# Moving single steps in the engines' order at seven places of a two-block, fp32-split transformer kernel

## What is computed

```python
gate_a, gate_b = jnp.split(jax.nn.sigmoid(gates + b_gate[l]), 2, axis=-1)       # block 1
merged = gate_a * (o_a @ w_proj_a[l]) + gate_b * (o_b @ w_proj_b[l])
...
u = rms_norm_2(h, mix_norm[l])                                                  # block 2, per layer
(z_s, xbc, dt_s, qkv, z_d, b_d, a_d, gate_s, gate_d) = jnp.split(u @ w_in[l], split_points, axis=-1)
y_s = mamba2_branch(z_s, xbc, dt_s, ...)     # softplus of dt_s, convolution, scan, gated norm
y_d = deltanet_branch(qkv, z_d, b_d, a_d, ...)   # l2_norm of q and k, delta rule, gated norm
merged = (jax.nn.sigmoid(gate_s) * (y_s @ ssm_w_branch[l])
          + jax.nn.sigmoid(gate_d) * (y_d @ dn_w_branch[l]))
```

## Time and profile before

| | us |
|---|---|
| runs: median (lowest, highest) | 2187.85 (2183.99, 2188.01) |
| the profiled execution, device time | 2184.31 |
| its span, first to last instruction | 2182.5 |
| TensorE busy | 2113.6 (97%) |
| TensorE weight loads busy | 1851.0 (85%) |
| VectorE busy | 1333.4 (61%) |
| ScalarE busy | 1150.2 (53%) |
| GpSimd busy | 67.8 (3%) |

### The profile page before, as it was taken

The page is one execution under the profiler, slowest core; times in us unless marked ns, Lnnn a source line. Parts: engine busy times, 40 slices in busy tenths (PEclk is TensorE's granted clock), DMA queues, the critical chain, the costliest instruction groups (busy, mean ns, idle before and its releaser), DMA issues.

```text
span 2182.5 us, 39373 instructions
## 1 busy us (share of the span) xinstructions
PE 2113.6 (97%) x15558; PEld 1851.0 (85%) x15558; DVE 1333.4 (61%) x1846; ACT 1150.2 (53%) x1713; POOL 67.8 (3%) x88
## 2 busy tenths in 40 slices
PE   7999999999999999989999999999999998999998
PEld 5888778888888988889998888888998888998887
DVE  3447565565557976667555556555897575756555
ACT  3554754454445576645445445444557663535444
POOL 1000000000000010100000000000001010000000
PEclk9999999999999999999999999999999999999999
DMA  9763255545554545322445555554454430355553
GB/s 389 297 235 117 97 181 192 185 165 201 183 191 138 190 151 176 120 79 86 180 180 200 190 181 187 186 181 156 171 177 152 156 118 37 141 188 189 182 188 125
DMA packets 53458, 373.09 MB, mean 171 GB/s; under 512 B 6320, under 2 KB 6448, under 8 KB 9424
## 3 DMA queue, kind: packets, MB, share of 16 engines
q1 hardware_dynamic: 47808, 342.00, 43.4%
q0 software_dynamic: 5520, 29.23, 3.9%
HBM read 370.10 MB, written 1.11 MB: 170 GB/s over the span
## 4 chain that ended last, share of the span: by engine, by line
PE 85%; DVE 6%; ACT 4%; issue 2%; DMA 1%; POOL 1%; SPq 0%; DVEq 0%; ACTq 0%; POOLq 0%
PE banks L558 14%; PE banks L560 13%; PE banks L559 13%; PE banks L511 9%; PE banks L513 9%; PE banks L512 9%; PE banks L614 4%; DVE LO L2139 2%; ACT HI L1524 1%; PE banks L668 1%; DMA ring<-in_w_stream 1%; PE banks L643 1%; PE banks L644 1%; PE banks L648 1%; PE banks L1298 1%
## 5 line engine op out<-in xcount | busy, mean ns | idle before, releaser
L1524 ACT ACTIVATE HI<-ring 128x1024 fp32r<-128x1024 f32 x606 | 625.8, 1055 | 717.0 <-PE banks L560 394.8
L2133 DVE TENSOR_TENSOR LO<-ring,HI 128x1024 fp32r<-128x1024 f32 x334 | 409.0, 1227 | 368.8 <-ACT HI L1524 368.5
L2139 DVE TENSOR_TENSOR LO<-ring,HI 128x2048 fp32r<-128x2048 f32 x134 | 307.3, 2293 | 206.7 <-ACT HI L1524 206.3
L511 PE MATMUL banks<-UH,HI 128*128 128x256 f32 x1456 | 423.7, 291 | 5.0 <-DVE LO L2139 5.0
L512 PE MATMUL banks<-UL,HI 128*128 128x256 f32 x1456 | 411.7, 283 | 0.0
L513 PE MATMUL banks<-UH,LO 128*128 128x256 f32 x1456 | 411.5, 283 | 0.0
L558 PE MATMUL banks<-HI,UH 128*128 128x512 f32 x896 | 349.1, 390 | 0.9 <-DVE UL L2146 0.9
L560 PE MATMUL banks<-HI,UL 128*128 128x512 f32 x896 | 348.7, 389 | 0.0
L559 PE MATMUL banks<-LO,UH 128*128 128x512 f32 x896 | 348.6, 389 | 0.0
L511 PEld LDWEIGHTS banks<-UH,HI 128*128 128x128 f32 x1456 | 278.6, 191 | 21.5 <-issue 14.9
L512 PEld LDWEIGHTS banks<-UL,HI 128*128 128x128 f32 x1456 | 278.9, 192 | 1.9 <-issue 1.7
(11 more groups left out here) (354 smaller groups left out, 2992.9 us busy)
## 6 DMA issues: line engine op xcount, KB each, us to landing
ring<-in_w_stream SPq DMA_DIRECT2D x315, 1024.0 KB, 4.8
ARENA<-in_ada_stream POOLq DMA_DIRECT2D x16, 1024.0 KB, 7.8
ARENA<-in_ada_stream SPq DMA_DIRECT2D x8, 1024.0 KB, 13.7
GRMS<-cum_rows POOLq DMA_DIRECT2D x16, 256.0 KB, 3.5
ARENA<-in_na_bias POOLq DMA_DIRECT2D x2, 1024.0 KB, 12.9
RMS<-cum_rows POOLq DMA_DIRECT2D x8, 256.0 KB, 3.6
RSTD<-cum_rows POOLq DMA_DIRECT2D x8, 256.0 KB, 3.7
ARENA<-in_ropes POOLq DMA_DIRECT2D x1, 1088.0 KB, 10.1
```

What stands on the lines that cost most here:

```text
L511: nc.tensor.matmul(out, lh, rh, start=start, stop=False, **kw)
L1524: nc.scalar.activation(HI[:, q % PARTS, at], ring[:, q % RING, at], ACT.Copy).then_inc(hi_ready, 1)
L2133: nc.vector.tensor_tensor(LO[:, q % PARTS, at], ring[:, q % RING, at], HI[:, q % PARTS, at].bitcast(F32), ALU.subtract).then_inc(lo_ready, 1)
L2139: nc.vector.tensor_tensor(LO[:, q % PARTS, :], ring[:, q % RING, :], HI[:, q % PARTS, :].bitcast(F32), ALU.subtract).then_inc(lo_ready, 2)
```

## The change

Seven stretches of the order are changed. No instruction is added or taken away; some stand elsewhere on their engine. Both layers of block 2 run the same code, so five of the seven occur twice.

```diff
@@ TensorE, block 1 @@
+            b1_half(14, 1)
             ada_columns(1)
-            b1_half(14, 1)
@@ ScalarE, block 1 @@
                     if k == 9:
                         open_gates(0, 5)
-                    if k == 10:
+                    if k == 11:
                         open_gates(5, 3)
-                    if k == 11:
-                        open_gates(8, 3)
             gate_rows(0)
             heads_high(2)
+            open_gates(8, 8)
             gate_rows(1)
-            open_gates(11, 5)
@@ ScalarE, mixer start (VectorE alike, between the product r_*e and the wait for Ln) @@
                 nc.scalar.activation(SMX[:, 7, 0:SP_COLS], pk2("a_log", 0, SP_COLS), ACT.Exp).then_inc(small_scalar, 1)
+                ahead(LQ_WIDE)
                 act.wait_ge(small_vector, 3 * l + 3)
@@ VectorE, convolution loop @@
                     for i in range(ROUND):
-                        split(Q_LAYERS + LQ_WIDE + i + PARTS, rounds + r)
                         convolve(ROUND * r + i, i % 2)
+                        split(Q_LAYERS + LQ_WIDE + i + 1 + PARTS, rounds + r)
@@ ScalarE, z panels @@
-                    if j in (3, 5):
-                        qk_root((j - 3) // 2)
+                    if j in (2, 5):
+                        qk_root(j // 4)
@@ VectorE, z panels @@
-                    if j in (3, 5):
-                        qk_reciprocal((j - 3) // 2)
                     if j >= 4:
                         qk_norm(j - 4)
+                    if j in (2, 5):
+                        qk_reciprocal(j // 4)
@@ VectorE, last gate panels @@
                 for j in range(4):
-                    scan_low(j)
-                    if j == 1:
+                    if j == 0:
                         dve.wait_ge(orms_ready, l + 1)
                         nc.vector.reciprocal(OROOT, OROOT).then_inc(or_ready, 1)
+                    scan_low(j)
...
+                    if j == 2:
+                        late_low(L_ZD + L_GATES - END_GATES + 2)
                 for j in range(4):
                     at = slice(2 * j, 2 * j + 2)
                     branch_low(8 + j, YDL[:, at, :], YDH[:, at, :], QKV[:, at, :])
-                    if j % 2:
-                        late_low(L_ZD + L_GATES - END_GATES + 2 + j // 2)
+                    if j == 3:
+                        late_low(L_ZD + L_GATES - END_GATES + 3)
```

More of the change, by code:

```diff
@@ L1857, in _ @@
                 for j in range(j0):
-                    ahead(LQ_WIDE + j)
+                    if j:
+                        ahead(LQ_WIDE + j)
                     conv_in(j, j % 2)
@@ L2638, in _ @@
                     for i in range(ROUND):
-                        split(Q_LAYERS + LQ_WIDE + i + PARTS, rounds + r)
                         convolve(ROUND * r + i, i % 2)
+                        split(Q_LAYERS + LQ_WIDE + i + 1 + PARTS, rounds + r)
                 def conv_panel(j):
-                    ahead(LQ_WIDE + j)
+                    if j > L_CONV - SCAN_CONV - ROUND:
+                        ahead(LQ_WIDE + j)
                     convolve_tile(j, j % 2, 0)
```

## The result

| | before | after |
|---|---|---|
| first set of runs: median (lowest, highest), us | 2185.92 (2183.52, 2188.01) | 2167.48 (2166.05, 2169.37) |
| ratio after to before, 95% interval | | 0.9917 [0.9903, 0.9932] |
| profiled execution: device time, span | 2184.31, 2182.5 | 2166.82, 2165.0 |
| TensorE busy, and span less busy | 2113.6, 68.9 | 2110.9, 54.1 |

The change makes the kernel 0.83% faster. (The kernel before has a lower median here than ahead of the prediction, since a fourth execution has joined the three.) Of the span's 17.5 us, 68.9 - 54.1 = 14.8 are idle time of TensorE and 2.7 are busy time, although its work is the same.

A forecast was written before the change was run, and what follows sets the result against it. The prediction took TensorE, busy 97% of the span, and its gaps as the bound. Gains of 2.85 us once and 4.98 per layer sum to 12.8 us (0.59%), giving 2173.5 us, range 2168.5 to 2180.

The forecast's parts named there:

- term 1: Modulation columns: 24 products of a half panel cover VectorE's copy TensorE waited for; gain 1.1 us, once.
- term 4: First q/k root: table load, root and reciprocal placed earlier, ending TensorE's 2.1 us wait; gain 2.1 us per layer.
- term 7: LO part of gate panel E4 on VectorE placed earlier, so TensorE starts E4 sooner; gain 1.44 us per layer.
- Term 3: Softplus: Ln and Sigmoid with their table loads go behind HI of c2, which starts earlier; gain 1.24 us per layer.
- Term 2: Gates: sigmoids moved later, so copies for value products and broadcast, and UL, come earlier; gain 1.75 us, once.
- term 6: Reciprocal of OROOT comes earlier, its 0.7 us wait goes, but TensorE waits 0.5 at E2; gain 0.2 per layer.
- term 5: Second q/k root: VectorE's reciprocal and norm product swapped, but the broadcast needs both; the 1.2 us wait stays, gain 0.
- successor was late: Rival: ScalarE's drain at c2 and the LO of P0 each come 0.8 us later; 2176.8 us, 17%.
- The convolution stayed TensorE's: Rival: the reordered loop's branch makes VectorE set the convolution's pace, 17.3 us lost; 2192.3 us, 2%.
- The swap: Rival: swapping reciprocal and product at the second q/k root gains 1.2 us twice; 2171.1 us, 6%.
- Longer low stretches: Rival: the clock's low stretches come out longer in three places by 1.7 us; 2178.6 us, 10%.
- the table loads at double cost: Rival: moved ScalarE table switches cost 2.56 us instead of 1.28, sum of gains 3.7; 2182.6 us, 1%.

The follow-up runs named there:

- fourth profile: The changed kernel with no edit, profiled in its fourth set of runs; that set gained 17.3 us, ratio 0.992 to the kernel before.
- best3: Changed kernel plus second root a z panel earlier, GpSimd's group 2 sum held back, E2's LO ahead of the scan's low parts; 0.9924 and 0.9917 to the kernel before.
- third set: The changed kernel with no edit, timed a third time; gained 17.4 us, ratio 0.9914 to the kernel before.

## Why the prediction was wrong

**What bounds the kernel** was right: each move that shortened a wait of TensorE brought its later products forward by as much, and a start that it gained was handed on through all later stages.

**Terms 1, 4 and 7** were forecast 1.1, 2.1 and 1.44 and measured 1.17, 2.19 and 1.44. **Term 3** (1.24 forecast, 1.25 measured) held, with the two loads at 1.28 each and no gap between a load and what follows, so that the Trainium skill's further 1.38 us per switch ("ScalarE: Activation LUTs", What ACT_TABLE_LOAD costs) appears nowhere in this trace. **Term 2** gave 1.95 for 1.75, **term 6** 0.27 for 0.2 with E2 waiting 0.3 and not 0.5, and **term 5** 0.04 for 0. Together 13.5 for 12.8: these sizes cost 0.7 us of the error. The idle time of TensorE bears the sum out by another way: 69.0 us as the mean of two profiles before, 55.4 of four after, so 13.5 (single profiles of the changed kernel lie between 54.1 and 57.6).

**The step that failed** is the one that the prediction put as "a few us on either side are luck". From it I took the sum of the waits as the whole gain, set the low-clock stretches as equally likely before and after, and gave their shortening no case of its own. Over all sets the kernel before has a mean of 2185.7 in 91 executions and the changed one 2167.9 in 19: 17.9 with a standard error of 0.5, 4.4 us over the waits. The mean granted clock of the changed kernel's runs is 0.9946, of the kernel before 0.9931. If every low stretch cost its full share, that is 0.0015 x 2170 = 3.3 us; going by the spread inside the sets, where 0.001 of clock goes with 1.3 us, it is 2 us (an estimate, from clocks rounded to 0.001). The base, 2186.3 in effect, was 0.6 too high; so 0.7 + 4.4 + 0.6 is, but for rounding, the whole distance of 5.6 from 2173.5 to that mean.

**Of the 4.4** the runs point to 1.8: TensorE's wait of 2.1 us for the first root was followed by a low stretch in 7 of 12 places, and without it in none. The stretches at the mixer's start, whose absence I read first, are not it: the fourth profile has one again in layer 0 and the third in both layers. For the other 2.6 us the runs give no place, and their cause stays open. Each part undone cost 2.5 to 3.3 us over its waits; alone, the same parts gave -1.0, 0.5 and 1.7, and terms 4 to 7 together 2.8. So the parts don't add up, and with sets of 5 or 6 executions whose means have a standard error of about 0.9 us I can't say whether that is an interaction or chance. best3 shows that it isn't a rule that fewer waits bring more clock. The Trainium skill ("TensorE: Matmul & The Clock Gate", Part 1) has the turn of the clock vary from run to run. That agrees for single executions (the same wait was followed by 0.50 in one profile and by 1.00 in another), but a mean over 19 executions moved with the order of the program.

**The rivals.** No successor was late where I feared it: c2 and P0 have no wait after the change, though P0's cover is thinner than the 0.25 worked out, since only 0.14 of the 0.56 gained at E2 in best3 got past it. One was late where I didn't look: the second broadcast, by 0.16, since I followed term 4's squares to TensorE and not past GpSimd and VectorE. The convolution stayed TensorE's. The swap did nothing. Longer low stretches came in one of the four profiles (third set).

**Three figures of the prediction** are off by its own working: the middle of 2171.5 and 2175.05 is 2173.3, the table loads at double cost leave a sum of 3.9 and not 3.7, and the convolution's 17.3 us are one layer's and would from the common base give 2190.8, not 2192.3. None of them changes how the forecast came out.

## What to carry over

A row of waits says who came last, and the sum of new starts less old ones gave each move's worth to within 0.2 us, where the durations were steady; that part can be trusted. A wait that has become shorter can be a wait moved: look whether the place before it has become later by as much. Ask also of a long wait (2.1 us here) whether a stretch of low clock ever follows it, look at several profiles before you say where the clock fell, and count the wait's end with what those stretches cost. Before moving a step into a gap of VectorE, look what GpSimd does there, and compare a candidate that removes the last small waits over ten executions: here 2.2 us of waits gone bought nothing.

## What was not expected of the hardware

- VectorE's product of two operands in SBUF took 1.79 us beside GpSimd's sum and 0.68 without it, and GpSimd's sum 2.04 and 1.30, in the runs with the second root at z4. The rows fit one running at a time: the sum starts at 895.80 during the LO part that ends at 896.69, and 896.6 + 1.3 = 897.9 is its end; the product, started at 896.61, ends at 898.40, about 0.6 after it. The Trainium skill ("SBUF — State Buffer", SBUF: two separate sides) says that such a VectorE instruction and one of GpSimd that reads SBUF take a shared pair of ports as a whole; the trace agrees.
- VectorE's product by the norm, with one operand in a bank, kept its 1.40 us beside GpSimd's second sum.
- TensorE's granted clock fell to half for some 3 us after a wait of 2.12 us in one profile and not after one of 2.11 in another, each behind products without a gap.
